# Constant products in five TensorE gaps, and VectorE block transposes in place of TensorE products, in a two-layer streaming encoder step

## The chip, the cores and the metric

One core of a Trainium2 chip runs the whole program as one launch. The metric is the device time of one execution in microseconds; the figure for the kernel before is the median of three runs.

## The reference, cut to what matters

One step of a two-layer encoder over 320 tokens: a prompt of 256 and a sample of 64, `D = 1024`. Layer 0 mixes with RWKV-7 and then runs a mixture of experts; layer 1 attends over a shared key/value and then runs its own mixture of experts. Every sub-layer normalises, scales and shifts the input with vectors that come from a conditioning vector `c`.

```python
def wkv_step(state, inp):                      # per head, 64x64 state, scanned over the tokens
    r, w, k, v, a, b = inp
    sa = jnp.einsum('bhvk,bhk->bhv', state, a)
    state = state * w[:, :, None, :] + sa[..., None] * b[:, :, None, :] + v[..., None] * k[:, :, None, :]
    return state, jnp.einsum('bhvk,bhk->bhv', state, r)
...
        mod = cs @ p['ada_w'][l] + p['ada_b'][l]
        sh1, sc1, g1, sh2, sc2, g2 = jnp.split(mod, 6, axis=-1)
...
        gu = jnp.einsum('sd,edf->sef', t, w_gu)         # 32 experts, the two best of one group per token
        hid = jax.nn.silu(gu[..., :D_EXPERT]) * gu[..., D_EXPERT:] * cw[..., None].astype(t.dtype)
        return jnp.einsum('sef,efd->sd', hid, w_down)
```

The kernel computes the scan in five chunks of 64 tokens (`NCH = 5`). Within a chunk it needs, per head, the inverse of a unit triangular 64x64 matrix.

## The kernel before, in words

Five engines run their own instruction streams, written out by hand, and meet at counting semaphores: `pe.did(ins, key)` counts an instruction, `ve.wait(key)` waits for that count, `settle()` makes an engine wait for its own last instruction. `Banks.open` (L233) hands TensorE the next of the eight PSUM banks in rotation, after waiting until the bank's last content was read. All ordinary products go through `mm` (L685), so they share the line L686 of the profile; transposes by TensorE have lines of their own.

**The inverse stage** (TensorE from L864 on, VectorE from L1645). Sixteen heads lie as 2 x 64 partitions by 8 column groups `c`, so that one "product per head" is a bank of sixteen 64x64 products (32 instructions in f32). First, chunk by chunk (`j`), TensorE makes the matrices of a chunk, `N1` among them, and turns three operands into token order. `tt` and `tmat` are the inverse and its transpose. They begin as the inverse of the 2x2 diagonal blocks and are doubled in levels `l = 2..6`; after level `l` the finished diagonal blocks are 2^l wide, so 32 after level 5. A level makes `W = nl^T tmat` for the five chunks, ScalarE copies it to `wmat`, and then for each chunk TensorE makes `TT` (what is added to `tt`) and `TW` (what is added to `tmat`), the last level `TT` alone. VectorE adds both and cuts the next level's `nl` out of `nt`.

**The modulation steps** run inside that stage. `mod_step(n)` (L707), 48 of them, multiplies a 1 MB slice of `ada_w` or `kv_ada_w` with the conditioning vectors. SyncE issues the slice's load into one of two buffers (L578) after step `n - 2` has used the buffer. Four steps belong to each chunk of the first part; in a level, pairs of steps follow the chunks 0, 2 and 4. They stand in TensorE's stream at those places, so a late slice stops the products behind it.

**The expert stage** `moe(l)` (L981 on TensorE) runs once per layer. In TensorE's order: `mean_square` (a product with ones, for the norm); the router's `logits`, which wait for the normalised chunks `h`; transposes `htok` and `logits tok`; then VectorE's routing, after which `mask` lets the small `rank` products start; VectorE then makes the picking matrices, and the `rows` products gather the tokens sorted by expert; VectorE counts the `passes` and picks each expert's slots; then the loop over the experts starts with `weights` and `gate_up`. After layer 0 `mean_square("A1")` (L1125) is followed by the key/value projection, which waits for its own normalised chunks.

Of the kernel before, what the change touches and what calls it, by code (L numbers as in the profile page):

```python
# [38 lines left out]
C = D // P  # L39
SEQ, DEC = 256, 64  # L40
T = SEQ + DEC
# [203 lines left out]
def build(nc, i, o, known, seen):  # L245
    ctx = ExitStack()
    with ctx:
# [432 lines left out]
        def _(eng):  # L680
# [38 lines left out]

            def mean_square(tag):  # L720

                pb = bank.open("ms", tag)
                for c in range(C):
                    if c % 2 == 0:
                        pe.wait("squares", tag, c // 2)
                    ins = mm(pb[:, 0:T], cst("ones"), sq_buf(tag)[:, c, :], c == 0, c == C - 1)
                full(ins, "ms", tag)
# [136 lines left out]
            for j in range(NCH):  # L864
# [13 lines left out]
                pb = bank.open("N1", j)  # L878
                for c in range(C):
                    ins = per_head(pb, slice(64 * c, 64 * c + 64), [(kk[:, c, t], aa[:, c, t])], c)  # L880
                full(ins, "N1", j)
# [7 lines left out]
            for l in range(2, 7):  # L889
# [7 lines left out]
                for j in range(NCH):  # L897
                    t = slice(CH * j, CH * (j + 1))
                    pe.wait("W ready", l, j)
                    pb = bank.open("TT", l, j)  # L900
                    for c in range(C):
                        ins = per_head(pb, slice(64 * c, 64 * c + 64), [(wmat[:, c, t], tt[:, c, t])], c)
                    full(ins, "TT", l, j)
                    if l < 6:
                        pb = bank.open("TW", l, j)
                        for c in range(C):
                            ins = per_head(pb, slice(64 * c, 64 * c + 64), [(tt[:, c, t], wmat[:, c, t])], c)
                        full(ins, "TW", l, j)
                    for n in steps_of_level(l, j):
                        mod_step(n)  # L910
# [70 lines left out]
            def moe(l):  # L981
                S = moe_sems[l]
                mean_square(f"B{l}")
                eng.wait_ge(in_sems[f"router_in{l}"], 32)
# [6 lines left out]
                for j, (t0, k) in enumerate(TILES):  # L991
                    for hf in range(2):
# [10 lines left out]
                        full(ins, "htok", l, j, hf)  # L1003
                pe.wait("mask", l)
# [7 lines left out]
                full(ins, "rank", l)  # L1012
                for hf in range(2):
                    for c in range(C):
# [10 lines left out]
                        full(ins, "rows", l, c, hf)  # L1025
                pe.wait("passes", l)
# [98 lines left out]
            mean_square("A1")  # L1125
            project("kv", range(4), hkv, lambda hf: ("wkv",), ("h", "KV"))
# [363 lines left out]
        def _(eng):  # L1490
# [154 lines left out]
            for j in range(NCH):  # L1645
# [8 lines left out]
                pb = pk("N1", j)[:, :].rearrange("p (c t) -> p c t", c=C)  # L1654
                ve.settle()
                tt_(tmat[:, :, t], pb, bmid(wcst("lev1n"), C), M, ("read", "N1", j))
                tt_(tt[:, :, t], nt[:, :, t], bmid(wcst("lev")[:, 0:64], C), M)
                ve.settle()
                tt_(tmat[:, :, t], tmat[:, :, t], bmid(cst("i64"), C), A_)
                tt_(tt[:, :, t], tt[:, :, t], bmid(cst("i64"), C), A_)  # L1660
                tt_(nl[:, :, t], nt[:, :, t], bmid(wcst("lev")[:, 64:128], C), M, ("level", 2, j))
                mods_out(range(A_STEPS * j, A_STEPS * (j + 1)))
                ve.settle()
            for l in range(2, 7):
                for j in range(NCH):
                    t = slice(CH * j, CH * (j + 1))
                    pb = pk("TT", l, j)[:, :].rearrange("p (c t) -> p c t", c=C)
                    if l < 6:
                        ve.wait("TW", l, j)
                    tt_(tt[:, :, t], tt[:, :, t], pb, A_, ("read", "TT", l, j), ("T ready", j), ("inverses",))  # L1670
                    if l < 6:
                        pb = pk("TW", l, j)[:, :].rearrange("p (c t) -> p c t", c=C)
                        tt_(tmat[:, :, t], tmat[:, :, t], pb, A_, ("read", "TW", l, j))
                        tt_(nl[:, :, t], nt[:, :, t], bmid(wcst("lev")[:, 64 * l:64 * l + 64], C), M,
                            ("level", l + 1, j))
# [350 lines left out]
```

## Time and profile before

| what | value |
|---|---|
| median of 3 runs | 1324.32 us (1315.74 to 1326.11) |
| the profiled execution | 1324.0 us, span 1321.8 us |
| mean granted TensorE clock | 0.938 of full speed |
| PE busy | 1131.9 us, 86% |
| DVE busy | 542.0 us, 41% |
| ACT busy | 341.3 us, 26% |
| the chain that ended last | PE 75%, DMA 11%, DVE 9% |

### The profile page before, as it was taken

How to read it: one execution, taken by the hardware profiler on the slowest of the kernel's cores; microseconds unless marked ns; L12 is line 12 of the kernel's file. 1: busy time of each engine (PE TensorE's matmuls, PEld its weight loads, DVE VectorE, ACT ScalarE, POOL GpSimd, SP SyncE). 2: the span in 40 equal slices, each digit the busy share in tenths (PEclk: the TensorE clock that was granted, in tenths of full speed). 3: DMA queues.
4: the chain of work that ended last, by engine and by line, in shares of the span. 5: the costliest groups of instructions: out<-in, count | busy, mean ns of one | idle time of the engine just before them, and what ended most of it. 6: DMA issues, size and time to landing. Idle time of an engine off the chain costs nothing.

```text
span 1321.8 us, 23637 instructions
## 1 busy us (share of the span) xinstructions
PE 1131.9 (86%) x9653; PEld 659.4 (50%) x9653; DVE 542.0 (41%) x1424; ACT 341.3 (26%) x650; POOL 56.4 (4%) x66
## 2 busy tenths in 40 slices
PE   5579998878887968689999999789795899999995
PEld 2146665556666935444444444567572534444433
DVE  3431194424341162624444444524337235444434
ACT  1112240121111211323233332234303233323322
POOL 2000000000000000000001000000000000000100
PEclk9789998999898979789999999899797999999997
DMA  8533115776775054009999996300622089999941
GB/s 249 171 127 121 71 64 177 277 258 238 259 261 205 4 221 191 1 10 425 421 425 425 423 417 249 135 12 1 255 103 89 0 349 423 428 426 420 422 199 40
DMA packets 45977, 297.21 MB, mean 225 GB/s; under 512 B 5956, under 2 KB 7336, under 8 KB 22344
## 3 DMA queue, kind: packets, MB, share of 16 engines
q1 hardware_dynamic: 43856, 290.17, 55.3%
q0 software_dynamic: 1840, 5.79, 1.9%
q8 instruction: 64, 1.05, 0.3%
q14 instruction: 17, 0.14, 0.0%
q10 hardware_dynamic: 200, 0.06, 0.0%
HBM read 293.77 MB, written 2.24 MB: 224 GB/s over the span
## 4 chain that ended last, share of the span: by engine, by line
PE 75%; DMA 11%; DVE 9%; ACT 2%; issue 2%; SPq 0%; ACTq 0%; DVEq 0%; POOL 0%; POOLq 0%
PE bank L686 73%; DMA ring<-in_ada_w 9%; DVE work L1501 2%; DMA ring<-in_kv_ada_w 2%; ACT work L1245 1%; DVE work L1507 1%; DVE work L1504 1%; DVE rstd L1539 1%; DVE x_res L1874 1%; DMA ring<-in_rw_w_rkv 1%; PE bank L1064 1%; DVE work L1860 1%; DVE ring L1501 1%; DVE work L1613 0%; PE bank L1231 0%
## 5 line engine op out<-in xcount | busy, mean ns | idle before, releaser
L686 PE MATMUL bank<-ring,work 128*64 128x512 f32 (+1 forms) x1760 | 351.3, 552 | 9.3 <-DVE work L1860 7.6
L686 PE MATMUL bank<-work,ring 128*128 128x320 f32 (+3 forms) x1600 | 302.0, 367 | 30.6 <-DVE work L1501 8.4
L686 PEld LDWEIGHTS bank<-work,ring 128*128 128x128 f32 (+2 forms) x1600 | 214.0, 173 | 118.5 <-issue 30.6
L686 PE MATMUL bank<-work 128*128 128x320 bf16 (+7 forms) x1906 | 227.0, 284 | 41.8 <-DVE work L1781 13.9
L686 PEld LDWEIGHTS bank<-ring,work 128*64 128x64 f32 (+1 forms) x1760 | 118.9, 138 | 218.3 <-issue 211.2
L686 PEld LDWEIGHTS bank<-work 128*128 128x128 bf16 (+3 forms) x1906 | 166.8, 126 | 113.2 <-issue 39.7
L1245 ACT ACTIVATE work<-bank 128x320 f32<-128x320 f32 (+6 forms) x111 | 55.8, 537 | 252.4 <-PE bank L686 235.8
L686 PE MATMUL bank<-ring 64*64 64x64 f32 (+2 forms) x2624 | 103.8, 233 | 2.1 <-issue 2.1
L686 PEld LDWEIGHTS bank<-ring 64*64 64x64 f32 (+2 forms) x2624 | 94.1, 144 | 21.8 <-issue 18.0
L686 PE MATMUL bank<-ring,cs 128*32 128x512 f32 x448 | 64.5, 661 | 39.9 <-DMA ring<-in_ada_w 33.9
L1874 DVE SCALAR_TENSOR_TENSOR x_res<-bank,mod,x_res 128x256 f32<-128x256 f32 (+1 forms) x256 | 86.1, 378 | 16.8 <-PE bank L686 2.7
L1854 DVE SCALAR_TENSOR_TENSOR work<-work,small,bank 128x256 f32<-128x256 f32 x32 | 21.5, 673 | 172.3 <-ACT work L1409 88.5
L1245 ACT ACTIVATE ring<-bank 128x512 f32<-128x512 f32 (+3 forms) x67 | 37.7, 563 | 194.5 <-PE bank L686 193.4
L1867 DVE TENSOR_TENSOR work<-bank,work 128x512 f32<-128x512 f32 x64 | 44.1, 689 | 61.9 <-ACT work L1413 61.9
L1501 DVE TENSOR_TENSOR ring<-ring,bank 128x512 f32<-128x512 f32 x45 | 29.1, 685 | 84.2 <-PE bank L686 84.2
L640 POOL TENSOR_TENSOR work<-work 128x512 bf16<-128x512 f32 x32 | 36.4, 1158 | 546.7 <-ACT work L1417 546.7
L1413 ACT ACTIVATE work<-bank 128x512 bf16<-128x512 f32 x64 | 38.1, 596 | 49.3 <-PE bank L686 49.3
L1507 DVE SCALAR_TENSOR_TENSOR work<-work,vec 128x320 f32<-128x320 f32 x56 | 27.0, 545 | 53.1 <-PE bank L686 52.8
L686 PEld LDWEIGHTS bank<-ring,cs 128*32 128x32 f32 x448 | 10.6, 113 | 67.7 <-DMA ring<-in_ada_w 45.8
L1397 ACT COPY work<-work 128x512 f32 x64 | 39.3, 623 | 14.2 <-issue 14.1
L1417 ACT ACTIVATE work<-work 128x512 bf16<-128x512 f32 x64 | 40.1, 626 | 8.6 <-DVE work L1867 8.6
L1245 ACT ACTIVATE work<-x_res 128x640 f32<-128x640 f32 x20 | 14.7, 737 | 98.5 <-DVE x_res L1507 46.0
(185 smaller groups left out, 754.3 us busy)
## 6 DMA issues: line engine op xcount, KB each, us to landing
ring<-in_moe_w_gu SPq DMA_DIRECT2D x64, 2048.0 KB, 13.5
ring<-in_moe_w_down SPq DMA_DIRECT2D x64, 1024.0 KB, 14.0
ring<-in_ada_w SPq DMA_DIRECT2D x40, 1024.0 KB, 5.3
ring<-in_rw_w_rkv SPq DMA_DIRECT2D x6, 2048.0 KB, 8.0
ring<-in_ada_w SPq DMA_DIRECT2D x4, 2048.0 KB, 28.6
ring<-in_kv_ada_w SPq DMA_DIRECT2D x8, 1024.0 KB, 4.9
ring<-in_rw_w_o SPq DMA_DIRECT2D x2, 2048.0 KB, 11.5
ring<-in_at_w_q SPq DMA_DIRECT2D x2, 2048.0 KB, 14.1
```

The costliest lines, as they stand in the source:

```text
L640: eng.tensor_tensor(dpart[:, 0, 2, cols], rest[:, n, :], dpart[:, 0, 1, cols], ALU.subtract).then_inc(S["lo_ready0"], 1)
L686: return eng.matmul(out, l, r, start=start, stop=stop, **kw)
L1064: ins = eng.transpose(ps[0][:, 2 * P * u + P * f:2 * P * u + P * f + P], hid[:, u, P * f:P * f + P], ident)
L1245: ac.did(eng.activation(out, in_, f, **kw), *keys)
L1397: eng.copy(xe[:, u, :, 64 * v:64 * v + 64], xall[:, :, bass.ds(at, SLOTS)]).then_inc(S["xe_ready"], 1)
L1413: eng.activation(dpart[:, u, 0, 512 * n:512 * n + 512], ps[4 + n][:, :], ACT.Copy).then_inc(S["hi_ready"], 1)
L1417: eng.activation(dpart[:, u, 1, 512 * n:512 * n + 512], rest[:, n, :], ACT.Copy).then_inc(S["mid_ready"], 1)
L1501: op(eng.tensor_tensor(out, a, b, o_), *keys)
L1507: op(eng.scalar_tensor_tensor(out, a, s_, b, o1, o2), *keys)
L1854: eng.scalar_tensor_tensor(hid_w[:, u], silu[:, u, :].rearrange("p (q f) -> p q f", f=2), wslot[:, u:u + 1], ps[3 + 4 * u][:, FE:2 * FE].r ...
L1867: eng.tensor_tensor(rest[:, n, :], ps[4 + n][:, :], dpart[:, u, 0, 512 * n:512 * n + 512], ALU.subtract).then_inc(S["rest_ready"], 1)
L1874: ins = eng.scalar_tensor_tensor(x[:, c, t0:t0 + n], ps[(6, 1, 2)[c % 3]][:, t0:t0 + n], mod[:, l, r, 40 + c:40 + c + 1], x[:, c, t0:t0 + ...
```

## The change

TensorE gets a helper `keep_busy(n)`: it opens a bank and makes `n` f32 products of the constant ones with the constants' first 320 columns, which nobody reads. It is called in four places of each expert stage (7 products after `mean_square`, 9 before the wait for `mask`, 6 after `rank`, 4 before the wait for `passes`) and once before the key/value projection (9).

In the inverse stage `N1` and the `TT` products of levels 2 to 5 go. VectorE makes the transposed matrix from the other one by its transpose of 32x32 blocks in place, as long as nothing but zeros lies outside those blocks: 5 transposes in the first part, 20 in the levels. `TW` of level `l` now waits for `turned`, the transpose after level `l - 1`. VectorE cuts `nl` before it adds `TW` and adds nothing to `tt` until level 6.

```diff
+            def keep_busy(n):
+
+                pb = bank.open("unused")
+                for _ in range(n):
+                    mm(pb[:, 0:T], cst("ones"), const[:, 0:T], True, True)
+                bank.owner[(bank.n - 1) % 8] = None
...
-                pb = bank.open("N1", j)
-                for c in range(C):
-                    ins = per_head(pb, slice(64 * c, 64 * c + 64), [(kk[:, c, t], aa[:, c, t])], c)
-                full(ins, "N1", j)
...
                     pe.wait("W ready", l, j)
-                    pb = bank.open("TT", l, j)
-                    for c in range(C):
-                        ins = per_head(pb, slice(64 * c, 64 * c + 64), [(wmat[:, c, t], tt[:, c, t])], c)
-                    full(ins, "TT", l, j)
+                    pe.wait("turned", l, j)
+                    if l == 6:
+                        pb = bank.open("TT", l, j)
+                        for c in range(C):
+                            ins = per_head(pb, slice(64 * c, 64 * c + 64), [(wmat[:, c, t], tt[:, c, t])], c)
+                        full(ins, "TT", l, j)
...
                 mean_square(f"B{l}")
+                keep_busy(7)
...
+                keep_busy(9)
                 pe.wait("mask", l)
...
                 full(ins, "rank", l)
+                keep_busy(6)
...
+                keep_busy(4)
                 pe.wait("passes", l)
...
             mean_square("A1")
+            keep_busy(9)
...
-                pb = pk("N1", j)[:, :].rearrange("p (c t) -> p c t", c=C)
-                ve.settle()
-                tt_(tmat[:, :, t], pb, bmid(wcst("lev1n"), C), M, ("read", "N1", j))
+                ve.settle()
                 tt_(tt[:, :, t], nt[:, :, t], bmid(wcst("lev")[:, 0:64], C), M)
                 ve.settle()
-                tt_(tmat[:, :, t], tmat[:, :, t], bmid(cst("i64"), C), A_)
-                tt_(tt[:, :, t], tt[:, :, t], bmid(cst("i64"), C), A_)
-                tt_(nl[:, :, t], nt[:, :, t], bmid(wcst("lev")[:, 64:128], C), M, ("level", 2, j))
+                tt_(tt[:, :, t], tt[:, :, t], bmid(cst("i64"), C), A_, ("turned", 2, j))
+                tt_(nl[:, :, t], nt[:, :, t], bmid(wcst("lev")[:, 64:128], C), M)
+                ve.settle()
+                op(eng.transpose(tmat[:, :, t], tt[:, :, t]), ("level", 2, j))
...
+                        tt_(nl[:, :, t], nt[:, :, t], bmid(wcst("lev")[:, 64 * l:64 * l + 64], C), M)
+                        tt_(tmat[:, :, t], tmat[:, :, t], pb, A_, ("read", "TW", l, j), ("level", l + 1, j))
+                        ve.settle()
+                        op(eng.transpose(tt[:, :, t], tmat[:, :, t]), ("turned", l + 1, j))
```

## Rows read from the trace of the kernel before

**Rows 1.** The page's chain of work that ended last, share of the span by engine.

```profile
PE 75%; DMA 11%; DVE 9%; ACT 2%; issue 2%; SPq 0%; ACTq 0%; DVEq 0%; POOL 0%; POOLq 0%
```

**Rows 2.** Busy time by stretch, layer 0's experts to key/value; after the engines the granted clock.

```profile
526.90:533.73 6.83, 5.21 (x10) 1.68 (x11) 6.55 (x20) 2.58 (x6) 0.00 (x0) 0.50 0.09 36
533.73:543.97 10.24, 5.13 (x34) 3.35 (x32) 5.27 (x26) 7.45 (x10) 0.00 (x0) 1.00 0.00 1
543.97:554.21 10.24, 4.56 (x17) 3.08 (x18) 9.58 (x44) 0.44 (x1) 0.00 (x0) 0.50 0.01 2
...
581.51:588.34 6.83, 6.27 (x18) 1.93 (x20) 1.08 (x7) 2.84 (x4) 0.00 (x0) 0.50 0.00 0
...
837.51:844.34 6.83, 3.56 (x7) 2.41 (x8) 6.76 (x18) 2.58 (x6) 0.00 (x0) 0.50 0.05 17
```

**Rows 3.** TensorE's timeline there: start, duration, line, operands, count, idle before.

```profile
518.36 4.47 PE L686 MATMUL bank<-work,const 128*128 128x320 f32 x16
528.42 7.25 PE L686 MATMUL bank<-work,router 128*36 128x320 f32 x16 [5.59 <-ACT work L1245]
...
536.90 1.96 PE L1002 MATMUL bank<-const,work 128*128 128x128 f32 x16
545.80 0.42 PE L686 MATMUL bank<-work 128*128 128x32 bf16 x9 [6.94 <-DVE work L1781]
550.08 28.12 PE L686 MATMUL bank<-work 128*128 128x320 f32 x96 [3.85 <-DVE work L1507]
581.12 0.23 PE L686 MATMUL bank<-work 128*128 128x6 bf16 x3 [2.92 <-DVE work L1837]
...
582.31 10.07 PE L686 MATMUL bank<-ring,work 128*64 128x512 f32 x32
```

**Rows 4.** VectorE's timeline of the same stretch.

```profile
529.08 2.82 DVE L1504 TENSOR_SCALAR work<-work,coef,mod 128x256 f32<-128x256 f32 x10
...
537.08 0.23 DVE L1720 COPY work<-bank 128x72 f32<-128x72 f32 x1 [2.39 <-PE bank L997]
```

**Rows 5.** TensorE's timeline, the first expert products of layer 1.

```profile
1053.04 8.52 PE L686 MATMUL bank<-ring,work 128*64 128x512 f32 x32
...
1063.49 7.09 PE L686 MATMUL bank<-ring,work 128*64 128x512 f32 x32
```

**Rows 6.** TensorE's timeline around the key/value projection.

```profile
829.17 4.57 PE L686 MATMUL bank<-work,const 128*128 128x320 f32 x16 [0.77 <-DVE x_res L1874]
840.78 19.22 PE L686 MATMUL bank<-work,ring 128*128 128x320 f32 x64 [7.04 <-DVE work L1504]
```

**Rows 7.** Busy time by stretch, the first and last of the levels 2 to 5.

```profile
289.62:316.41 26.79, 22.80 (x536) 17.36 (x532) 9.57 (x17) 3.58 (x6) 0.00 (x0) 0.94 0.64 227
...
367.41:393.22 25.81, 22.17 (x536) 15.86 (x532) 9.89 (x18) 3.58 (x6) 0.00 (x0) 1.00 0.73 259
```

**Rows 8.** Chain of waits in the levels: start, duration, what the chain ran through.

```profile
299.79 7.58 DMA ring<-in_kv_ada_w
...
326.17 8.12 DMA ring<-in_ada_w
...
352.37 6.73 DMA ring<-in_ada_w
...
385.30 6.88 DMA ring<-in_ada_w
```

**Rows 9.** Groups by form, 289.62 to 414.6: count, busy us, mean ns, idle before.

```profile
L686 PE MATMUL bank<-ring 64*64 64x64 f32 x2240 | 74.9, 229 | 2.1 <-issue 2.1
...
L1501 DVE TENSOR_TENSOR ring<-ring,bank 128x512 f32<-128x512 f32 x45 | 29.1, 685 | 84.2 <-PE bank L686 84.2
```

**Rows 10.** TensorE's timeline in the inverse stage's first part, modulation steps after a wait.

```profile
226.99 1.94 PE L686 MATMUL bank<-ring,cs 128*32 128x512 f32 x8 [2.86 <-DMA ring<-in_ada_w]
...
258.62 1.06 PE L686 MATMUL bank<-ring,cs 128*32 128x512 f32 x8 [1.88 <-DMA ring<-in_ada_w]
...
273.88 1.07 PE L686 MATMUL bank<-ring,cs 128*32 128x512 f32 x8 [1.64 <-DMA ring<-in_ada_w]
```

More of the change, by code:

```diff
@@ L1666, in _ @@
                     t = slice(CH * j, CH * (j + 1))
[L1667 to L1671, printed above, removed]
+                    if l == 6:
+                        pb = pk("TT", l, j)[:, :].rearrange("p (c t) -> p c t", c=C)
+                        tt_(tt[:, :, t], tt[:, :, t], pb, A_, ("read", "TT", l, j), ("T ready", j), ("inverses",))
+                    else:
                         pb = pk("TW", l, j)[:, :].rearrange("p (c t) -> p c t", c=C)
-                        tt_(tmat[:, :, t], tmat[:, :, t], pb, A_, ("read", "TW", l, j))
-                        tt_(nl[:, :, t], nt[:, :, t], bmid(wcst("lev")[:, 64 * l:64 * l + 64], C), M,
-                            ("level", l + 1, j))
+                        tt_(nl[:, :, t], nt[:, :, t], bmid(wcst("lev")[:, 64 * l:64 * l + 64], C), M)
+                        tt_(tmat[:, :, t], tmat[:, :, t], pb, A_, ("read", "TW", l, j), ("level", l + 1, j))
+                        ve.settle()
+                        op(eng.transpose(tt[:, :, t], tmat[:, :, t]), ("turned", l + 1, j))
                     mods_out(steps_of_level(l, j))
```

## The prediction

> **What bounds the kernel now.** I read the chain of waits first: three quarters of the span run through TensorE and a ninth through DMA [rows 1]. So the time is TensorE's, and the question for every edit is which stretch it shortens and what ends that stretch. The loop over the experts is not touched; what is left are the gaps around it and the inverse stage.
>
> In the gaps I read the granted clock by stretch, then TensorE's timeline. After `mean_square` TensorE idles 5.59 us until the first normalised chunk, and the products that follow stand at 0.50; the same happens after the 6.94 us before `rank`, after the 3.85 us before `rows` and after the 2.92 us before `weights` [rows 2, 3]. The clock is lost in the gap and paid for behind it: the 16 `logits` instructions take 7.25 us, where 16 of the same 320 columns at full clock took 4.47; the first `gate_up` takes 10.07 us in layer 0 and 8.52 in layer 1, where the next such group took 7.09 [rows 3, 5].
>
> In the inverse stage I read the levels' busy time and the chain there. Levels 2 to 5 run from 289.62 to 393.22, 25.9 us each, with TensorE busy for 22 to 23 [rows 7]. But the chain goes through the loads of the modulation steps in each level [rows 8]: a pair of steps frees both buffers, and the second load of the next pair is the late one. TensorE is nearly full there, yet a load ends many of its waits.
>
> **The constant products.** One f32 product is two instructions of 4.47 / 16 = 0.279 us, so 0.56 us at full clock [rows 3].
>
> Seven after `mean_square`: 14 x 0.279 = 3.9 us in a 5.59 us gap, 1.7 us idle left. They delay nothing, since the normalisation covers them; without that cover they would cost 3.9 us. What they buy: VectorE's ten scalings end at 529.08 + 2.82 = 531.9 [rows 4], and seven products behind the one at 529.7 end at 529.7 + 7 x 0.56 = 533.6 at full clock, against 528.42 + 7.25 = 535.67. That is 2.0 us, and it is passed on, because VectorE's routing (537.08) waited for TensorE [rows 4].
>
> Nine before `mask`: 18 x 0.279 = 5.0 us in 6.94, 1.9 left. Six after `rank`: 3.35 us in 3.85, 0.5 left. What they buy: `rows` starts at 550.08 and runs at half clock until 554.21 [rows 2, 3], 4.13 us that hold 2.07 us of work. If the clock drops while the six run, they end up to 1.2 us after the pick (3.35 plus about 1.7 lost, against 3.85), leaving 0.9; all six at half clock would take 6.7, leaving 2.07 - 2.85 = -0.8.
>
> Four before `passes`: 2.2 us in 2.92, 0.7 left, and the register read of `passes` behind them on TensorE may slip by 0.1. They buy 10.07 - 7.09 = 2.98 us in layer 0 and 8.52 - 7.09 = 1.43 in layer 1 [rows 3, 5], 4.4 in all.
>
> Nine before the key/value projection: 5.0 us in 7.04 [rows 6], 2.0 left. They buy at most half of the 3.56 us that the projection ran at half clock [rows 2], 1.8.
>
> How much of this holds depends on the idle that is left. Rows of such waits: after 1.64 and 1.88 us the step ran in 1.06 to 1.07 us; after 2.86 in 1.94, at half clock [rows 10]. The 0.7 us before `weights` are far under that: I take 4.2 of the 4.4. The 1.7 (with another wait behind the first `logits` product), 1.9 and 2.0 us lie near or between these rows, so I take about midway between a kept and a lost clock: 1.2 for `logits` (0.3 to 2.0), 1.4 for `rows` (-0.8 to 2.1), both twice, and 1.0 for the projection (0 to 1.8). Sum 2.4 + 2.8 + 4.2 + 1.0 = 10.4 us; all kept 14.4, clock lost behind each of the three but not under the products 6.6.
>
> Opening banks for them shifts the rotation. The banks' last readers are done by then (the four take that of an early `rows` product), so I cost it at nothing.
>
> **The inverse stage.** A product per head is 32 instructions of 74.9 / 2240 = 0.033 us, 1.07 us of TensorE [rows 9]. `N1` removes five. They stand between pairs of steps whose loads TensorE then waits for, 1.6 to 2.9 us each [rows 10], so they are worth nothing; without those waits 5.4 us. `TT` removes twenty, 21.4 us of work, which is not 21.4 us of time. In a level, three pairs of steps: the second load takes about 8.1 us after a pair whose loads were issued together and 6.8 after a staggered one [rows 8], plus a 1.06 us step. With one `TW` per chunk the work between pairs is at most five `W` and one `TW`, 6 x 1.07 = 6.4 us, less than a load. So a level becomes 8.1 + 6.8 + 6.8 + 3 x 1.06 = 24.9, against 25.9: 4 x 1.0 = 4.0 us. What is late next is the load again. TensorE is then idle about 8 us per level instead of 4 [rows 7], so more steps meet half clock at +0.88 us each [rows 10]. I count four more, half of them hidden: -1.5. I take 2.5 us. Bounds: 8.8 if all three pairs are staggered (23.7 per level), -6.6 if one step of each of the twelve pairs runs at half clock more than now.
>
> VectorE loses thirty instructions of 0.69 us and gets 25 transposes, which no row shows. Nearest rows are its 128x512 additions at 0.685 [rows 9]; I take 0.69, since they move the same elements. The Trainium skill, VectorE: DVE Perf Modes, section The three transpose paths, gives 311 ns for 128x128 in bf16; four of those would be an estimated 1.2 us, and the sum would be the same. It is the same because `turned` has slack: a chunk's transpose ends about 2.1 us after its `TW`, while the next level's first `TW` stands behind a pair of steps and five `W`. Behind the waiting `TW` stand the pair of steps and with them SyncE's next load. VectorE's level, 5 x (2 x 0.685 + transpose), passes 24.9 only when a transpose takes over 3.6 us.
>
> **Sum.** 10.4 + 2.5 = 12.9 us off the profiled execution's 1324.0, which is the median within 0.3: 1311. Rounding towards the stagger that I left out, **1310.5 us**.
>
> **Rivals.** (1) Everything pays: every gap keeps its clock and all pairs stagger, 14.4 + 8.8 = 23.2, so 1301. For it, `mean_square`, the same product form, holds full clock; against it, the idle that is left behind three of them. (2) The gains are eaten: the clock falls behind three gaps and the level stage loses 3 to thin work at half clock, 6.6 - 3 = 3.6, so 1320.5. For it, the wait of 2.86 us that cost the clock. (3) The other side: the block transposes are slow and VectorE bounds the levels. Place: TensorE waiting for `level` and `turned`; it decides from 3.6 us per transpose. At 5 us a level takes 5 x 6.4 = 32, 6 more than now, 24 in four, so 1324.0 - 10.4 + 24 = 1338. No row speaks for so slow an operation. (4) The products do not hold the clock at all: they fit their gaps, nothing is bought, 1321.5. (5) TensorE's transposes leave it at half clock, and the nine products before `mask` start so: 18 x 0.56 = 10 us in 6.94, `rank` 3 us late twice, 10.4 - 6 + 2.5, so 1317. The rows speak against: the 16 transposes end at 538.86 and the clock stays at 1.00 until 543.97, 5.1 us on [rows 2, 3]. The Trainium skill, TensorE: Matmul & The Clock Gate, section Part 4: PE-mode transpose, says that the full clock does not engage for transposes, which do not count as busy in the same way. The trace disagrees with that here.
>
> **How the numbers follow.** Forecast 0.50, its own range 1305 to 1316; rival 1 0.20; 2 0.19; 3 0.05; 4 0.03; 5 0.03. The range takes the forecast with most of rivals 1, 2 and 5: 1300 to 1320. A measurement of this kernel tells about 1% from no change, so faster by that means below 1311.1: all of rival 1 and six tenths of the forecast, 0.50. Slower by over 1% is rival 3 and a little for what I did not see, 0.06. The rest, 0.44, is within 1%.
>
> **What would show it.** Right: `gate_up` at 7.1 us in both layers; `rows` near 26 us and `logits` shorter in at least one layer; levels near 25 us with chain pieces through the loads as before; transposes under 1.3 us. Wrong: constant products at 0.56 us per instruction; `rank` or `rows` waiting for TensorE instead of VectorE; levels at 26 us or more, or a wait for VectorE before `TW`.

## The result, and the profile after

The kernel after took 1301.79 us in the median of four runs (1300.34 to 1308.81), the one before 1323.71 in the same comparison: ratio 0.9846, 95% interval 0.9804 to 0.9888. Six further runs gave 1301.0, ratio 0.983 [0.9798, 0.9863]. The forecast was 1310.5 with a range of 1300 to 1320: the time lies in the range, near its fast end, where the first rival stood (1301). The sum behind the forecast took 12.9 us off; 22 came off, so the time lies inside by the width that rival gave the range. The profiled execution took 1300.34 us, span 1298.6, mean granted clock 0.949 against 0.938.

The chain of waits, by engine, answers to [rows 1] and hardly differs:

```profile
PE 75%; DMA 11%; DVE 8%; ACT 3%; issue 2%; SPq 0%; ACTq 0%; DVEq 0%; POOL 0%; POOLq 0%
```

**The gaps.** TensorE's timeline of layer 0's expert stage in the kernel after, to be held against [rows 3] (start, duration, line, operands, count, idle before):

```profile
508.56 3.93 PE L686 MATMUL bank<-const 128*128 128x320 f32 x14
514.33 0.70 PE L686 MATMUL bank<-work,router 128*36 128x320 f32 x2 [1.83 <-ACT work L1255]
515.68 3.96 PE L686 MATMUL bank<-work,router 128*36 128x320 f32 x14 [0.65 <-DVE work L1514]
...
520.87 1.97 PE L1008 MATMUL bank<-const,work 128*128 128x128 f32 x16
522.67 5.01 PE L686 MATMUL bank<-const 128*128 128x320 f32 x18
529.86 0.39 PE L686 MATMUL bank<-work 128*128 128x32 bf16 x9 [2.18 <-DVE work L1790]
530.10 5.17 PE L686 MATMUL bank<-const 128*128 128x320 f32 x12
535.10 26.00 PE L686 MATMUL bank<-work 128*128 128x320 f32 x96
560.94 2.32 PE L686 MATMUL bank<-const 128*128 128x320 f32 x8
564.03 0.23 PE L686 MATMUL bank<-work 128*128 128x6 bf16 x3 [0.77 <-DVE work L1846]
...
565.22 8.78 PE L686 MATMUL bank<-ring,work 128*64 128x512 f32 x32
```

The instructions out of `const` are the constant products; 14, 18, 12 and 8 of them stand where TensorE idled. The `logits` end 10.9 us after `mean_square` instead of 12.8, `rows` takes 26.00 us instead of 28.12. But the six products behind `rank` took 5.17 us, not 3.35, and `rows` follows them with no wait for VectorE; and the first `gate_up` is still not at 7.09. The granted clock by stretch shows why, the answer to [rows 2] (the column before the last two):

```profile
502.50:531.28 28.78, 24.12 (x113) 15.60 (x112) 19.24 (x70) 11.32 (x18) 0.95 (x1) 1.00 0.28 110
531.28:534.70 3.42, 3.42 (x8) 2.25 (x7) 3.24 (x11) 0.00 (x0) 0.00 (x0) 0.50 0.00 0
534.70:565.41 30.71, 29.21 (x114) 20.29 (x115) 10.18 (x45) 6.41 (x13) 0.00 (x0) 1.00 0.00 1
565.41:568.83 3.42, 3.42 (x10) 1.03 (x9) 0.45 (x3) 1.84 (x3) 0.00 (x0) 0.50 0.02 5
821.41:824.83 3.42, 3.42 (x8) 2.18 (x7) 3.38 (x14) 0.00 (x0) 0.00 (x0) 0.50 0.00 0
```

What half clock is left in layer 0's stage lies behind the idle that the products left: 2.18 us ahead of `rank`, and the two short waits around `passes` (0.77 and 0.66 us). At 821.41 it falls on the key/value projection, behind 2.19 us of idle. Layer 1's first `gate_up` is clean, against [rows 5]:

```profile
1029.50 7.09 PE L686 MATMUL bank<-ring,work 128*64 128x512 f32 x32
```

**The inverse stage.** Levels 2 to 5 by stretch (us, PE, PEld, DVE, ACT, POOL busy, then granted clock, DMA share, GB/s), against [rows 7]:

```profile
285.29:308.89 23.60, 20.47 (x376) 14.02 (x372) 9.80 (x17) 3.58 (x6) 0.00 (x0) 0.78 0.67 231
308.89:331.44 22.55, 16.02 (x372) 10.51 (x368) 9.90 (x17) 2.99 (x5) 0.00 (x0) 1.00 0.86 300
331.44:355.14 23.70, 18.00 (x377) 11.57 (x373) 9.92 (x17) 3.58 (x6) 0.00 (x0) 0.93 0.75 258
355.14:378.38 23.24, 19.17 (x377) 12.19 (x373) 10.02 (x17) 3.58 (x6) 0.00 (x0) 0.85 0.74 266
```

They take 23.3 us each (93.1 / 4) instead of 25.9. Of the third of them, the chain of waits without its pieces of issue (0.04 us or less each), against [rows 8]:

```profile
330.45 7.81 PE bank L686 x208
338.25 0.59 PE bank L704 x4
338.84 1.04 PE bank L686 x8
339.89 7.24 DMA ring<-in_ada_w
347.18 1.98 PE bank L686 x8
349.17 4.93 DMA ring<-in_ada_w
```

The first pair's loads are hidden under the five `W` and a `TW`; the second pair waits for a load of 7.24 us, the third for one of 4.93. The groups by form, against [rows 9], show the products that are gone and the transposes that came:

```profile
L686 PE MATMUL bank<-ring 64*64 64x64 f32 x1600 | 55.2, 231 | 0.5 <-issue 0.5
...
L1684 DVE STREAM_TRANSPOSE ring<-ring 128x512 f32<-128x512 f32 x20 | 14.2, 712 | 0.7
```

**Where the time went**, by stretches cut at the same events in each trace. The first part runs from the first A product to the start of step 19, the stage of the levels from there to the start of step 47; a gap from the end of `mean_square` to the end of the first `gate_up`, or to the end of the projection.

| us | before | after | after again |
|---|---|---|---|
| ahead of the inverse stage | 210.5 | 208.1 | 210.2 |
| first part | 78.1 | 76.2 | 74.3 |
| levels | 119.7 | 110.3 | 112.8 |
| to the end of layer 0's `mean_square` | 114.5 | 114.1 | 111.8 |
| gap, layer 0 | 69.5 | 65.3 | 64.3 |
| gap, key/value | 26.1 | 26.0 | 26.0 |
| attention | 133.8 | 132.0 | 133.8 |
| gap, layer 1 | 67.9 | 64.9 | 63.3 |
| both expert loops and the tail | 501.7 | 501.7 | 501.6 |

Two profiles of the same kernel differ by up to 2.5 us in a stretch, so a single pair of traces sizes no part by itself; the experiments give each part several times over.

### The profile page after: what moved, and what is told of

It reads as the page before. It is cut to its first block, busy times and chain, and to the rows that moved or that the text cites. A ratio compares the mean times of both kernels' runs of the same rounds, so it can differ in the third digit from the quotient of the medians.

```text
span 1298.6 us, 22252 instructions
## 1 busy us (share of the span) xinstructions
PE 1134.0 (87%) x8975; PEld 655.4 (50%) x8975; DVE 540.4 (42%) x1419; ACT 341.0 (26%) x650; POOL 56.4 (4%) x66
## 4 chain that ended last, share of the span: by engine, by line
PE 75%; DMA 11%; DVE 8%; ACT 3%; issue 2%; SPq 0%; ACTq 0%; DVEq 0%; POOL 0%; POOLq 0%
PE bank L686 73%; DMA ring<-in_ada_w 10%; DVE work L1511 2%; ACT work L1255 2%; DMA ring<-in_kv_ada_w 1%; DVE work L1517 1%; DVE work L1514 1%; DVE rstd L1549 1%; DVE x_res L1883 1%; DMA ring<-in_rw_w_rkv 1%; PE bank L1073 1%; DVE work L1869 1%; DVE ring L1511 1%; DVE work L1623 0%; PE bank L1241 0%
## 5 line engine op out<-in xcount | busy, mean ns | idle before, releaser
L686 PE MATMUL bank<-ring,work 128*64 128x512 f32 (+1 forms) x1600 | 342.9, 582 | 9.3 <-DVE work L1869 7.6
L686 PE MATMUL bank<-work 128*128 128x320 bf16 (+7 forms) x1906 | 223.6, 283 | 20.3 <-DVE x_res L1883 7.7
L686 PEld LDWEIGHTS bank<-ring,work 128*64 128x64 f32 (+1 forms) x1600 | 113.3, 137 | 212.0 <-issue 205.0
L686 PEld LDWEIGHTS bank<-ring 64*64 64x64 f32 (+2 forms) x1984 | 74.5, 146 | 25.4 <-issue 21.7
L686 PE MATMUL bank<-ring 64*64 64x64 f32 (+2 forms) x1984 | 84.3, 237 | 3.5 <-issue 3.5
L1511 DVE TENSOR_TENSOR ring<-ring,const_phase 128x512 f32<-128x512 f32 x30 | 20.4, 679 | 58.5 <-PE bank L686 58.3
## 6 DMA issues: line engine op xcount, KB each, us to landing
ring<-in_moe_w_down SPq DMA_DIRECT2D x64, 1024.0 KB, 14.2
```

Source lines behind the costliest of these rows:

```text
L686: return eng.matmul(out, l, r, start=start, stop=stop, **kw)
L1511: op(eng.tensor_tensor(out, a, b, o_), *keys)
```

## The experiments

Theory A of the first experiments: the two parts add up, products in the gaps and shorter levels, the latter because the loads come apart. Single runs of the kernel before went from 1314.98 to 1331.81 us, so of an experiment timed in one run the trace is read, and the time decides little.

**The products alone**: the kernel before with `keep_busy` in its five places.

```diff
+                keep_busy(7)   # and 9, 6, 4 in moe; 9 before the projection
```

> The kernel before with the constant products alone; the inverse stage as before. Theory A (the two parts add, and the larger one is the shorter inverse stage): from the last mean_square instruction to the end of the first gate_up, layer 0 took 65.3 us with the whole change and 69.6 before, layer 1 64.9 and 67.9, and the key/value projection gained 0.1, so the constant products are worth 4.3 + 3.0 + 0.1 = 7.4 us: about 1316. Levels 2 to 5 stay near 103 us in all. Theory B (the stage got shorter by chance of the clock, and the constant products bring the gain): 1302 to 1306, like the whole change.

Measured: 1312.36 us, ratio 0.9917 [0.9889, 0.9945]. The gaps 65.3, 26.0 and 64.9 us, the levels 119.0. The gaps are those of the kernel after to within 0.1, the levels those of before. The time lies between theory A's 1316 and theory B's 1302 to 1306; the stretches are theory A's.

**The inverse stage alone**: the kernel after without any `keep_busy`.

```diff
-                keep_busy(7)   # and all the others
```

> The whole change without any constant product. Theory A: levels 2 to 5 take 93 us in all as in the changed kernel, the first part about 2 us less than before, so 12 us off the kernel before: about 1311. Theory B: levels near 103 us, 1320 or more. The prediction's own term for this part was 2.5 us, 1321.

Measured: 1311.07 us, ratio 0.991 [0.9875, 0.9946]. The levels 111.3, the gaps 68.3, 26.1 and 67.9. The two ratios give 11.0 and 11.9 us of 1322.93, 22.9 together, against 22 to 23 for both at once: the parts add up, as far as intervals of some 4 us either way tell.

**More products.**

```diff
-                keep_busy(7)
+                keep_busy(10)
...
-                keep_busy(9)
+                keep_busy(12)
...
-                keep_busy(4)
+                keep_busy(5)
...
-            keep_busy(9)
+            keep_busy(12)
```

> The changed kernel with fuller gaps: 10 products after mean_square, 12 before mask, 6 after rank, 5 before passes, 12 before the key/value projection; each product is 0.56 us, and the idle left in the changed kernel's gaps was 1.8, 2.2, 0.8 and 2.2 us, so all still fit at full clock. Theory A (what was not won in the gaps was lost to the clock falling in the idle that the products left): the clock stays at full through all of them; the projection loses 1.7 us, gate_up of layer 0 goes from 8.8 to 7.1, rows starts 1 us earlier in both layers, logits of layer 1 shortens by 1.5, together about 6 us off the changed kernel: near 1296. Rival (the clock falls for another reason, or the longer blocks run at half clock and overrun their gaps): 1300 to 1306, with idle before mask or h gone and TensorE late.

Measured: 1301.44 us, ratio 0.9832 [0.9773, 0.989]. The gaps took 62.6, 24.3 and 62.4. Layer 0's stretch in that trace, clock in the same column, and its `rank`, `rows` and `gate_up`:

```profile
500.00:575.00 75.00, 72.14 (x300) 46.41 (x298) 34.38 (x130) 20.31 (x33) 0.95 (x1) 1.00 0.12 45
```

```profile
534.18 3.48 PE L686 MATMUL bank<-const 128*128 128x320 f32 x12
538.12 26.11 PE L686 MATMUL bank<-work 128*128 128x320 f32 x96 [0.47 <-DVE work L1517]
...
568.35 7.09 PE L686 MATMUL bank<-ring,work 128*64 128x512 f32 x32
```

With the idle filled the clock stays at 1.00 through the stage, the six products take 3.48 us and `rows` waits for VectorE again. All three gaps together are 14.2 us under those of before, where the prediction's "all kept" was 14.4. The time, though, missed theory A's 1296 and was not shown to be better than the kernel after's: it lies in the rival's 1300 to 1306, without the rival's signs.

**Single steps in place of pairs.**

```diff
-LEVEL_STEPS = (2, 0, 2, 0, 2)
+LEVEL_STEPS = (1, 1, 1, 1, 2)
```

> The changed kernel with one modulation step behind each of the chunks 0 to 3 of a level and two behind chunk 4, in place of pairs behind chunks 0, 2 and 4. Theory A (a load that is issued within 1 us of the other takes 7.6 to 8.1 us, one that has the queue nearly to itself 4.8 to 5.0, so what shortens a level is that the two buffers are released apart): loads are issued apart, land in about 5 us, and a level goes from 23.3 us to about 20, near TensorE's own work: 10 us off the changed kernel, about 1291. Rival (the bytes per second of the loads bound the level, whichever way they are issued): levels stay at 23 us, 1300 to 1303.

Measured: 1311.32 us, ratio 0.9909 [0.9882, 0.9936]; the levels 117.9. Theory A missed here, and so did the rival: the levels grew. Loads released apart are not enough. The two loads that stand under the five `W` are waited for in no level, but of the other four steps of a level nearly every one now waits for its own load. TensorE's waits for modulation loads in the stage came to 27.6 us, 24.9 in the kernel after.

**Both loads waited for.**

```diff
+                    if n >= A_STEPS * NCH and n % 2 == 0 and n + 1 < MSTEPS:
+                        eng.wait_ge(in_sems[f"modw_in{(n + 1) % 2}"], 16 * ((n + 1) // 2 + 1))
```

> The changed kernel with one wait added: from step 20 on, the first step of a pair of modulation steps waits until the loads of both steps of its pair have landed, as it in effect did before, when the work between the pairs was long enough for both. No work of TensorE is added. Read are the four level stages from step 19's end to step 47's end, 110.3 us in the changed kernel and 119.7 before. Theory A (the levels got shorter because a pair's first step now runs as soon as its own load is there, which sets the two next loads 3 to 4.7 us apart, and a load issued so takes 4.8 to 5.5 us instead of 6.7 to 8.1): without the stagger the loads take 7 to 8 us again, the levels come to 25 to 27 us, the stage to 118 to 125 us, and the run to 1306 to 1313. Rival B (the levels got shorter by the removed work of TensorE alone, the order of the loads is a bystander): a pair that waits for its second load anyway loses only the 1.06 us step that it could have run meanwhile, partly, so at most 2 us over the stage: 110 to 112.5.

Measured: 1330.11 us in one run (the kernel before 1317.87 beside it); the levels 142.4. Both sizes are missed, rival B's 110 to 112.5 and theory A's 118 to 125: the wait goes further than the kernel before did, where the first step of a pair still ran when its own load had landed. The stage, and TensorE's waits in it (us in total, times, longest):

```profile
283.84:426.20 142.36, 91.50 (x1773) 57.54 (x1776) 41.95 (x69) 16.72 (x28) 0.00 (x0) 0.83 0.57 205
```

```profile
PE bank L686 <- DMA ring<-in_ada_w: 46.1, 12, 5.9
PE bank L686 <- DMA ring<-in_kv_ada_w: 7.6, 2, 4.8
```

So it shows that exposing both loads of a pair costs some 30 us. It does not measure the stagger alone, and so does not decide between A and B.

**The products put back.** The twenty `TT` again on TensorE, into banks that nobody reads.

```diff
+                    pb = bank.open(*(("TT", l, j) if l == 6 else ("unused",)))
+                    for c in range(C):
+                        ins = per_head(pb, slice(64 * c, 64 * c + 64), [(wmat[:, c, t], tt[:, c, t])], c)
...
+                    else:
+                        bank.owner[(bank.n - 1) % 8] = None
```

> The changed kernel with the twenty products of levels 2 to 5 put back on TensorE at their old places, into banks that nobody reads; VectorE keeps its new work with the twenty block transposes. Theory A (the products' 21 us of TensorE time are what the stage got shorter by, in part directly and in part because the pairs then find both loads landed and issue the next two together): the stage from step 19 to step 47 goes back to 117 to 121 us from 110.3, the run to 1305 to 1309. Rival C (VectorE's shorter list, two additions fewer per chunk and no wait for two products, is what made the levels shorter): the stage stays at 110 to 113.

Measured: 1319.15 us in one run, more than the 1305 to 1309 of theory A; the levels 121.7, just above its 117 to 121, against 119.7 and 119.0 in the two traces that have `TT`. Rival C is out: with VectorE's new list (one addition fewer per chunk, not two, and a transpose) and TensorE's old work the stage is as long as before.

**Every transpose four times.**

```diff
+                        for _ in range(3):
+                            op(eng.transpose(tt[:, :, t], tmat[:, :, t]))
+                            ve.settle()
```

> The changed kernel with each of the twenty block transposes of the levels done four times, the same transpose each time, one after the other. One took 0.71 us, so VectorE gets about 2.5 to 3 us more per chunk with the waits between them: a level of VectorE's comes to about 5 x (1.37 + 2.9) = 21 us. Theory A (the transposes have slack; only from about 3.6 us per chunk, when VectorE's level passes TensorE's, do they set the level): the stage stays at 110 to 113 us, the run within 3 us of the changed kernel. Rival D (the transposes are on the path: the first product of the next level waits for the last chunk's transpose): each level longer by up to 2.9 us for the last chunk, or by 5 x 2.9 if VectorE bounds, so 120 us or more for the stage.

Measured: 1303.47 us in one run; the levels 111.1. VectorE's busy time in the stage is twice the kernel after's (83.59 against 41.71 us) and the stage did not move: rival D is out.

```profile
286.19:397.29 111.10, 87.97 (x1774) 57.88 (x1774) 83.59 (x129) 16.72 (x28) 0.00 (x0) 0.87 0.74 261
```

**The pairs balanced.**

```diff
+                    if j == 2:                       # behind the third W
+                        for n in steps_of_level(l, 0):
+                            mod_step(n)
...
-                    for n in steps_of_level(l, j):
+                    for n in steps_of_level(l, {0: 2, 4: 4}.get(j, 1)):
```

> The changed kernel with the pairs of modulation steps moved within a level: one after the third W, one after the first TW, one after the last TW. So 3, 3 and 4 products of 1.07 us stand between the pairs, instead of 6, 2 and 2. No work is added or taken out. Theory A (a level is the sum of the waits for loads over what work covers them: the six products hide the first pair's loads with some to spare, the two products of the other pairs leave 2.8 to 5 us of waiting each): from one pair to the next it takes about the first step, 1.06, and a load of 5 to 6.5 us, so a level comes to 18.5 to 22.5 us instead of 23.3 and the stage to 95 to 107 us, the run to 1287 to 1298. A bound: in the level from 308.89 the DMA engines were busy for 0.86 of the time at 300 GB/s, so the loads can't do a level in less than about 0.86 x 22.55 = 19.4 us. Rival E (the loads together set the levels, whatever the order: the DMA engines' rate is the bound already): no change, the stage at 109 to 112 us.

Measured: 1303.86 us in one run; the levels 107.4, just outside theory A's 95 to 107 and below rival E's 109 to 112. The later kernel with the same placing took 100.0 there (below). Both speak for A; but the two differ by 7.4 us with the same code in that stage, at mean granted clocks of 0.90 and 0.95, so one trace does not size it, and the run's time missed A's 1287 to 1298.

**The kernel after once more.**

> The changed kernel once more, unaltered, timed beside the two that follow. The nine profiles so far give the first part of the inverse stage (first A product to step 19's end) 73.2 to 80.5 us with the same code in seven of them, so a single profile says little of what the five removed N1 are worth there. Theory A (the changed kernel's gains are the levels, some 8 us, and the gaps, some 7 us; the rest of a profile's difference is the place at which the clock's falls meet the work): the levels 109.5 to 112.5 us, the two expert gaps 63 to 66 us each, the first part anywhere in 73 to 81, the median 1298 to 1306. Rival (the removed N1 shortened the first part too, by 1.9): the first part again within 0.5 of 76.2.

Measured: 1301.0 us, ratio 0.983 [0.9798, 0.9863]; the levels 112.8, just over the expected 112.5; the first part 74.3, not within 0.5 of 76.2. That the removed `N1` shortened the first part is not shown: eleven traces without `N1` and with full loads have 72.9 to 80.5 us there, 76.3 in the mean, the two with it 77.8 and 78.1.

**More products, timed again.**

> The changed kernel with 10, 12, 6 and 5 constant products in the expert stage and 12 before the key/value projection in place of 7, 9, 6, 4 and 9. In one profile it kept the clock through all the gaps and took 149.3 us in them against 156.2, yet its time was not shown to differ. Theory A (the gain is real and 5 to 7 us, hidden before by the scatter of single runs): the median 1294 to 1298, 4 to 8 us below the changed kernel's of this same call. Rival F (what the gaps give is taken back elsewhere, since the falls of the clock come somewhere else): within 2 us of it.

Measured: 1297.84 us, ratio 0.9808 [0.9772, 0.9843]; gaps 149.3 us in all, as in its first profile. Its median is 3.2 us under the kernel after's beside it, and the intervals overlap: between theory A's 4 to 8 and rival F's 2, not settled.

**Everything together**: more products, balanced pairs, and four more groups of constant products.

```diff
+            keep_busy(5)
             pe.wait("y rstd")
             head_spread("y rstd all", heads)
+            keep_busy(9)
             project("wo", range(C), rr, lambda hf: ("wo", hf), ("mix out",))
...
+                if s == C:
+                    keep_busy(6)
+                elif s == C + 1:
+                    keep_busy(4)
                 if s >= 3:
                     prob_turn(s - 3)
```

> The fuller constant products, the pairs of modulation steps balanced within a level (after the third W, the first TW and the last TW), and constant products in four more waits where the profile shows TensorE idle and then at half clock: 5 before the wait of 3.3 us and 9 before the wait of 4.8 us around the output projection of layer 0, 6 and 4 before the waits of 4.2 and 3.1 us at the end of the attention. Theory A (each piece adds up): levels 106 to 109 us (-3), gaps 149.3 (-7), the stretch around the output projection up to 5 us and the end of the attention up to 5 us shorter, so 1281 to 1293. Rival F (falls of the clock only move to other places): 1297 or more.

Measured: 1278.99 us in the median of six runs (1273.7 to 1281.64), ratio 0.9661 [0.9629, 0.9692]. It beats both kernels: 44.8 us under before, 22.0 under after, and its interval lies clear of the kernel after's. It came out below theory A's range. The levels' stretch of its profile:

```profile
282.20:382.23 100.03, 80.55 (x1709) 53.12 (x1709) 39.75 (x67) 16.61 (x28) 0.00 (x0) 0.95 0.83 296
```

Against the other six-run profile with fuller products: levels 9.4 us less, first part 1.5, the stretch ahead of it 1.7, end of the inverse stage to `mean_square` 1.6, attention 2.4; the gaps the same 149.3. Each of these comes from one pair of traces, and the pieces were not timed one by one, so none but the whole is sized. The products before the output projection bought less than the 5 us allowed, and its timeline shows why:

```profile
447.03 5.11 PE L686 MATMUL bank<-const 128*128 128x320 f32 x18
451.98 0.70 PE L686 MATMUL bank<-work,ring 128*128 128x320 f32 x2
454.42 1.34 PE L686 MATMUL bank<-work,ring 128*128 128x320 f32 x4 [1.75 <-DVE work L1520]
455.99 1.34 PE L686 MATMUL bank<-work,ring 128*128 128x320 f32 x4 [0.23 <-DVE work L1520]
457.56 1.34 PE L686 MATMUL bank<-work,ring 128*128 128x320 f32 x4 [0.23 <-DVE work L1520]
```

The projection's first products, now at full clock, wait for VectorE chunk by chunk.

**Half the bytes.**

```diff
-                eng.dma_start(mw[n % 2], src[P * (n % C):P * (n % C) + P, 2048 * blk:2048 * (blk + 1)]
+                eng.dma_start(mw[n % 2][:, 0:1024], src[P * (n % C):P * (n % C) + P, 2048 * blk:2048 * blk + 1024]
...
-                    ins = mm(pb[32 * n:32 * n + 32, :], cs[:, c, :], w[:, 512 * n:512 * n + 512], c == 0, c == C - 1,
+                    ins = mm(pb[32 * n:32 * n + 32, :], cs[:, c, :], w[:, 512 * (n % 2):512 * (n % 2) + 512], c == 0, c == C - 1,
```

> The changed kernel with modulation loads of half the size: only the first 1024 columns of each slice are loaded, and the products of the second half read them again, so TensorE has as many products as before. It leaves out half of every slice (the modulation vectors, and what is routed behind them, are others), so only the inverse stage is read. Theory A (in the changed kernel the loads, not TensorE's work, are what a level's time comes from: pairs of steps wait for them): with half the bytes a load takes about 3 us and most waits go, a level falls from 23.3 to 17.5 to 20 us, near its ten products per head and six steps, 10 x 1.07 + 6 x 1.06 = 17.1, and the stage from 110 to 82 to 95. Rival G (the levels are bound by the order of TensorE, ScalarE and VectorE, W to copy to TW to VectorE, and the loads only fill the waits): the stage 105 to 112.

Measured in the inverse stage alone: the levels 91.9 us, the first part 60.0 where the other traces without `N1` have 72.9 to 80.5. Rival G is out. The stretch and the waits in it:

```profile
269.07:361.00 91.93, 78.56 (x1773) 53.14 (x1773) 41.60 (x69) 16.72 (x28) 0.00 (x0) 0.98 0.51 162
```

```profile
PE bank L686 <- DMA ring<-in_ada_w: 11.4, 12, 1.5
PE bank L686 <- DMA ring<-in_kv_ada_w: 2.9, 3, 1.0
```

The loads are what is late next, in the levels and in the first part, as the prediction had it. A level still took 19.4 us, from first pair to first pair, not 17.1, with 14.3 us of short waits for loads left in the stage: they fell from 24.9 by less than half, where most were expected to go.

## Why the prediction was right, and where its sizes were off

**The constant products, 10.4 us forecast.** Eight traces with the same 7, 9, 6, 4 and 9 products and whole loads have 152.8 to 156.2 us in the three gaps, 154.7 in the mean; the two without any have 163.5 and 162.3: 8.3 us, with 7.4 in the pair of before and after. The mechanism held, and so did "the clock is lost in the gap and paid for behind it". By terms, the mean of the eight against the trace of before, the forecast in brackets: `logits` 1.3 and 1.1 us (1.2 twice); `rows`, from the start of `rank` to its end, 1.5 and 1.3 (1.4 twice); `gate_up` 2.1 and 1.4 (4.2 together); the projection 0.3 (1.0). The last is the term that was wrong, and `gate_up` in layer 0 was taken too surely: of the eight traces four have 8.78 us there and four 7.09.

The values "about midway between a kept and a lost clock" came out as means of two outcomes. Behind the same idle the clock was kept in one place and lost in another, even within the kernel after: layer 0's `logits` ran their last fourteen instructions in 3.96 us behind 1.83 us of idle, layer 1's in 5.51 behind 1.82.

```profile
977.33 0.70 PE L686 MATMUL bank<-work,router 128*36 128x320 f32 x2 [1.82 <-ACT work L1255]
978.68 5.51 PE L686 MATMUL bank<-work,router 128*36 128x320 f32 x14 [0.65 <-DVE work L1514]
```

Over both layers of the eight traces the `logits` kept it in 8 of 16 cases, the six products behind `rank` in 4 of 16, behind 2.16 to 2.19 us of idle each time, and the projection in 1 of 8, behind 2.19. Which case keeps it is open. The two waits of about 0.77 and 0.66 us around `passes`, shorter than the waits of [rows 10] behind which the clock held, kept it in four traces of the eight and lost it in four. In the three traces with more products, where no single wait left is over 0.7 us, it was kept at every one of these places. In the kernel after `rows` follows the six products with no wait for VectorE, by the very course the prediction allowed for, the clock falling under the six; that `rows` waits for TensorE was also set down as a sign of being wrong, and it came.

**The inverse stage, 2.5 us forecast: the step that failed.** The prediction put a level at "8.1 + 6.8 + 6.8 + 3 x 1.06 = 24.9, against 25.9: 4 x 1.0 = 4.0 us", less 1.5 for half clock. The levels' stage is 119.7 and 119.0 us in the two traces of the old stage and 109.4 to 112.8, mean 111.2, in five of the new one: 8.2 us, near the upper bound that the prediction gave for all pairs staggered (8.8, 23.7 per level; measured 23.3 in the kernel after, 23.6 in the mean of the five). Two slips in these sums change nothing: half of four steps at 0.88 is 1.8, not 1.5, and three loads of 6.8 with their steps are 23.6 a level, not 23.7.

The mis-sized term is the load of the last pair. From the end of one pair's second step to the end of the next one's, the levels of the kernel after took 8.7, 8.5 and 6.0 us in the mean, where the sum has 9.2, 7.9 and 7.9. In the level shown above the first pair's loads were covered by work (8.4 us from 331.44 to the end of its steps) and the second pair's took 7.24, with a step at half clock behind it; but the last took 4.93, not 6.8, and it was 4.8 to 5.0 in all four levels. It was issued 3.0 to 4.7 us after its partner. In the levels of before and after a second load took 6.4 to 8.5 us when it was issued 0.9 us behind its partner, 6.5 to 6.9 at about 2 us, and 4.8 to 5.5 at 3 us or more.

The 6.8 came from [rows 8], where only loads stand that ended a wait. The trace of before had short last loads too, 4.9 to 5.4 us in three of its four levels, issued 3.4 to 4.0 us apart; they stood under two `TT` and two `TW` and ended no wait. One of them, issued behind the step at 334.33, in TensorE's timeline, then its load (the last number is the time from issue to landing, us):

```profile
334.33 1.06 PE L686 MATMUL bank<-ring,cs 128*32 128x512 f32 x8 [2.95 <-DMA ring<-in_ada_w]
335.32 5.50 PE L686 MATMUL bank<-ring 64*64 64x64 f32 x128
340.75 1.92 PE L686 MATMUL bank<-ring,cs 128*32 128x512 f32 x16
```

```profile
ring<-in_ada_w SPq DMA_DIRECT2D x1, 1024.0 KB, 5.4
```

So in the last pair the removed work uncovered a load that was mostly short already. With it falls "6 x 1.07 = 6.4 us, less than a load": in three levels of the kernel after the first pair's second load took 4.8 to 5.2 us and hid under that work. The loads of the other pairs changed their distances as well, and no run separates the two.

The books of the stage, kernel after against before. TensorE lost 20 x 1.07 = 21.4 us of work, but its busy time fell only from 101.35 to 86.29, as the granted clock went from 0.95 to 0.89: the other 6.3 us are put down to half clock. Its waits for the modulation loads grew from 17.1 to 24.9, 7.8 more, and the remainder (other idle, and ends of products that are modelled) shrank by 2.0. 21.4 - 6.3 - 7.8 + 2.0 = 9.3, the difference of the two stretches. So the prediction's shape was right, "21.4 us of work, which is not 21.4 us of time"; the loads took less of it back than forecast, the clock more. The two stretches, before and after:

```profile
288.62:408.30 119.68, 101.35 (x2413) 75.51 (x2413) 40.30 (x69) 16.72 (x28) 0.00 (x0) 0.95 0.69 247
```

```profile
284.29:394.63 110.34, 86.29 (x1772) 56.77 (x1772) 41.71 (x69) 16.72 (x28) 0.00 (x0) 0.89 0.74 262
```

**N1 at nothing** is not contradicted: the first part's scatter of over 7 us is larger than any difference. Halved loads shortened it by some 16 us, so it waits for loads at least in part.

**The transposes at 0.69 us, with slack up to 3.6**: 0.71, and four in a row per chunk did not lengthen the stage. No product of the levels waited for VectorE in the kernel after. The Trainium skill's 311 ns (VectorE: DVE Perf Modes, The three transpose paths) had given an estimated 1.2 us; the trace is well under it, and the sum would not have changed.

**The rivals.** The time is that of "everything pays", 1301, by another mix: the staggering of that rival, but not its clock kept in every gap, and some 5 us that belong to neither part. The measured terms, 8.3 and 8.2, sum to 16.5 of the 22 us; the rest lies in stretches whose scatter from trace to trace is as large (the first part, the stretch ahead of it, the attention), and stays open. The gains were not eaten, the transposes bounded nothing, and the products held the clock where they left little idle. The rival on TensorE's transposes is out: behind 24 of them (the line L1008) the nine products ahead of `mask` ran 18 instructions in 5.01 us, the clock at 1.00. The Trainium skill's sentence in TensorE: Matmul & The Clock Gate, Part 4: PE-mode transpose, that full clock does not engage for transposes, does not hold in the kernel after either: the clock was at 1.00 ahead of them and stayed there. Whether it would rise under transposes alone no run shows.

**The chances.** Faster by over 1% was given 0.50 and came true. The 0.44 on "within 1%" followed from the 2.5 us.

## What to carry to other kernels

In a stretch where loads and work alternate, read what each load takes against how far it was issued from its neighbour, and where the work that covers it stands. A chain of waits shows only the loads that came late: before taking work away, read the loads under that work too. Fill a TensorE gap up to the wait: idle of 0.7 us or less kept the clock at every place in the three traces with more products, while about 2 us kept it in some cases and lost it in others with the same code. Size a part of a change from several traces of the same code before explaining a difference of two or three microseconds.

## What the runs showed of the hardware that was not expected

- VectorE's 32x32 block transpose of a 128x512 f32 operand took 0.712 us, 0.711 when repeated at once; the additions of the same shape take 0.680.
- A 1024 KB load of `ada_w` took 5.0 us from issue to landing in the median of the kernel after, one of 512 KB 4.0 in the kernel with halved loads. The Trainium skill, DMA: Bandwidth & Descriptors, section Anatomy of one DMA — SWDGE (gpsimd) path, gives about 2.0 us plus the bytes at 436 GB/s, for loads that GpSimd issues: an estimate of 4.4 and 3.2. The step from one size to the other agrees (1.0 against 1.2), the rest is here, with SyncE as issuer and at times a second load in flight, 0.6 to 0.8 us longer.
- The DMA engines' mean rate in the same levels went from 247 GB/s (before) to 262 (after) and 296 (balanced pairs, fuller products) with the same bytes to move in a shorter time.
